# Half of the last projection tile put in front of the last attention's turning, and three conversions on other places of their queues

## The reference, cut to what matters

```python
def first_block(x, ...):                       # two layers
    for l in range(2):
        proj = rmsnorm(x, mix_norm[l]) @ w_in[l]         # retention, forgetting attention, RWKV, gates
        rwkv_c = rwkv_c + (prev - rwkv_c) * mu           # a difference with the position before
        x = x + merged(y_ret, y_fox, y_rwkv, gates) @ w_out[l]
        x = x + swiglu(rmsnorm(x, ffn_norm[l]))

def second_block(x, ...):                      # two layers, 13 groups of 256 projected columns
    for l in range(2):
        z = rmsnorm(x, norm_g[l]) @ w_in[l]
        o_a = axial rotary attention; o_b = windowed attention with a sink
        o_c = neighbourhood attention with a bias; o_d = difference of two softmaxes, rotary
        x = x + concat(o_a*silu(g_a), o_b*silu(g_b), o_c*silu(g_c), o_d*silu(g_d)) @ w_out[l]
    return rmsnorm(x, final_g)
```

## Time and profile before

| | us |
|---|---|
| median of 3 runs | 1119.23 (1119.02 to 1119.77) |
| the profiled execution | 1118.7 |
| its span in the trace | 1116.9 |
| PE busy in the span | 1102.8 |
| mean granted clock of PE | 0.997 |

### The profile page before, as it was taken

The page is one execution under the profiler, slowest core; times in us unless marked ns, Lnnn a source line. Parts: engine busy times, 40 slices in busy tenths (PEclk is TensorE's granted clock), DMA queues, the critical chain, the costliest instruction groups (busy, mean ns, idle before and its releaser), DMA issues.

```text
span 1116.9 us, 21111 instructions
## 1 busy us (share of the span) xinstructions
PE 1102.8 (99%) x8842; PEld 976.2 (87%) x8842; DVE 812.8 (73%) x1184; ACT 575.0 (51%) x858; POOL 85.3 (8%) x67
## 2 busy tenths in 40 slices
PE   9999999999999999999999999999999999999997
PEld 7789998999999998889998989999898778887786
DVE  6887664968666676888655968667677778877775
ACT  6465434444444445466444354444446676756763
POOL 1003100200000001112101200000000110002000
PEclk9999999999999999999999999999999999999998
DMA  9653335455345345443344355535345435354331
GB/s 356 233 199 102 143 116 190 152 226 226 150 190 225 136 163 218 151 152 114 115 143 168 145 227 226 208 136 220 150 150 194 155 142 187 121 197 148 115 112 38
DMA packets 29792, 188.23 MB, mean 169 GB/s; under 512 B 3537, under 2 KB 6353, under 8 KB 8337
## 3 DMA queue, kind: packets, MB, share of 16 engines
q1 hardware_dynamic: 26096, 175.63, 42.1%
q10 hardware_dynamic: 3232, 8.68, 2.1%
q0 software_dynamic: 384, 2.79, 0.7%
HBM read 181.84 MB, written 5.24 MB: 168 GB/s over the span
## 4 chain that ended last, share of the span: by engine, by line
PE 83%; issue 8%; DVE 3%; DMA 2%; ACT 2%; DVEq 1%; POOL 1%; POOLq 0%; SPq 0%; ACTq 0%
PE bank L712 14%; PE bank L772 13%; PE bank L1188 13%; PE bank L1206 10%; PE bank L1189 7%; PE bank L1165 4%; PE bank L1147 4%; DMA ring<-w_in_dram 2%; PE bank L1191 2%; PE bank L1331 1%; PE bank L864 1%; PE bank L700 1%; PE bank L727 1%; PE bank L880 1%; PE bank L903 1%
## 5 line engine op out<-in xcount | busy, mean ns | idle before, releaser
L712 PE MATMUL bank<-in_high,h_parts 128*128 128x512 f32 x544 | 177.4, 396 | 0.0
L772 PE MATMUL bank<-h_parts,in_high 128*128 128x256 f32 x768 | 144.9, 289 | 0.0
L712 PE MATMUL bank<-in_low,h_parts 128*128 128x512 f32 x336 | 131.5, 391 | 0.0
L712 PEld LDWEIGHTS bank<-in_high,h_parts 128*128 128x128 f32 x544 | 102.2, 188 | 23.9 <-issue 2.3
L772 PEld LDWEIGHTS bank<-h_parts,in_high 128*128 128x128 f32 x768 | 119.0, 191 | 3.2 <-issue 1.4
L1206 PEld LDWEIGHTS bank<-act_split,down_split 128*128 128x128 f32 x960 | 117.8, 191 | 0.9
L1206 PE MATMUL bank<-act_split,down_split 128*128 128x256 f32 x960 | 118.1, 283 | 0.0
L1188 PE MATMUL bank<-h_parts,up_split 128*128 128x512 f32 x308 | 110.6, 398 | 0.0
L1188 PE MATMUL bank<-h_parts,gate_split 128*128 128x512 f32 x308 | 110.3, 396 | 0.2
L772 PE MATMUL bank<-h_parts,in_low 128*128 128x256 f32 x384 | 108.4, 282 | 0.0
L1510 ACT ACTIVATE in_high<-ring 128x2048 fp32r<-128x2048 f32 x46 | 87.6, 1908 | 39.0 <-PE bank L712 31.9
(11 more groups left out here) (384 smaller groups left out, 2408.2 us busy)
## 6 DMA issues: line engine op xcount, KB each, us to landing
ring<-w_in_dram SPq DMA_DIRECT2D x70, 1024.0 KB, 4.9
ring<-w_gate_up_dram SPq DMA_DIRECT2D x44, 1024.0 KB, 7.7
ring<-w_down_dram SPq DMA_DIRECT2D x22, 1024.0 KB, 4.8
ring<-w_out_dram SPq DMA_DIRECT2D x16, 1024.0 KB, 4.8
ring<-p_all_dram SPq DMA_DIRECT2D x6, 1024.0 KB, 4.8
x_kept<-scratch ACTq DMA_DIRECT2D x4, 1024.0 KB, 3.9
ring<-w_in_dram SPq DMA_DIRECT2D x4, 512.0 KB, 7.2
scratch<-x_kept ACTq DMA_DIRECT2D x2, 1024.0 KB, 5.7
```

The source lines that it names most:

```text
L712: last = mm(bank[(n - n % 2 + t) % 4][:], a, b, start=c == 0 and i == 0, stop=c == KT - 1 and i == 2)
L772: last = mm(bank[g % 4][:, half * 256:(half + 1) * 256], a, b, start=k == 0 and i == 0, stop=k == KT - 1 and i == 2)
```

## The change

Four edits, all of them places in hand-written lists: in the first block, ACT's rounding of tile 5 comes behind the copies of groups 2 and 3 instead of ahead of them, and DVE's low part of tile 5 comes behind `projected_low(1)`. In the second block's third attention, a call of `piece` for blocks 0 and 1 of piece 25 is put ahead of `turn`, and the later call asks for blocks 2 to 7. In the difference attention, `out_low(2, 1)` goes to where `out_low(3, 0)` was, and `out_low(3, 0)` and `out_low(3, 1)` behind the attention; one block of piece 30 is moved behind `weigh(3)`; `next_half(0, 0)` is moved behind the low part of the last mix.

```diff
@@ PE, attend
                     weigh(3)
+                    if n == 2:
+                        piece(l, p + 4, range(2))
                     after()
                     values(1)
-                    piece(l, p + 4)
+                    piece(l, p + 4, range(2 if n == 2 else 0, KT))
@@ PE, the difference attention
                 values(2)
-                piece(l, 30, range(2))
+                piece(l, 30, range(1))
                 weigh(3)
-                piece(l, 30, range(2, 4))
+                piece(l, 30, range(1, 4))
@@ ACT, group of the first block
-                if g < 11:
+                if g < 11 and g != 3:
                     in_split(l, g + 2, ring_in, in_hi)
...
                         last.then_inc(g_out.sem, 2)
+                        if g == 3:
+                            in_split(l, g + 2, ring_in, in_hi)
@@ DVE, first block
                 projected_low(0)
-                in_split(l, 5, in_hi, in_lo)
...
                 projected_low(1)
+                in_split(l, 5, in_hi, in_lo)
@@ DVE, the difference attention
-                attention(l, att, 12, 8, 2, None, splits={1: lambda l: mixed_low(2), 5: lambda l: out_low(2, 1), 7: lambda l: out_low(3, 1)},
-                          mixing={5: lambda l: out_low(2, 0), 7: lambda l: out_low(3, 0)})
+                attention(l, att, 12, 8, 2, None, splits={1: lambda l: mixed_low(2)},
+                          mixing={5: lambda l: out_low(2, 0), 7: lambda l: out_low(2, 1)})
...
                 tt(g8, g8, put(st[:, 330:394], 1, 8), ALU.mult)
+                out_low(3, 0)
                 dve.wait_ge(*att.y.after(l, 4))
...
                 tt(y8, y8, put(st[:, 236:244], 2, HD), ALU.mult).then_inc(b_mix.sem, 1)
-                next_half(0, 0)
+                out_low(3, 1)
                 dve.wait_ge(*mx_hi.after(l, 4))
                 stt(mix_low[3][:], ...).then_inc(mx_lo.sem, 1)
+                next_half(0, 0)
                 next_half(0, 1)
```

## The result

| | before | changed |
|---|---|---|
| median, 18 runs each | 1119.12 us (1117.67 to 1119.90) | 1121.32 us (1120.62 to 1122.60) |
| profiled execution / its span | 1118.7 / 1116.9 | 1120.84 / 1119.0 |
| PE's instructions | 8842 | 8890 |

The ratio is 1.0023, with a 95% interval of 1.0017 to 1.0029: slower by 1.9 to 3.2 us. The result lies at the low end of the range that was forecast, 1121.4 to 1124.3. That range was counted from the earlier median of 1119.23: the new median is 0.08 us under it, and by the ratio the result is inside (1119.23 x 1.0023 = 1121.8). Lines of the changed kernel are a few further down: L1985 is L1989, L2020 is L2024, L2044 is L2048, L2144 is L2148, L2619 is L2623.

The account below looks back on a forecast made before the run. PE bounds the kernel, busy 1102.8 of 1116.9 us. The terms 4.38 + 0.53 - 0.18 - 0.94 - 0.07 = +3.7 us on the median 1119.23 gave 1122.95, put at 1123.0; range 1121.4 to 1124.3 for 8 in 10.

Parts of the forecast that it names:

- The bound and the sign: PE's list bounds the kernel; piece 25 computed twice adds matmuls, count 8842 to 8890, so the change is slower.
- The step that reads `token_major` as taking no blocks: Piece 25 in the third attention: both calls run the whole tile, adding 2.19 us a layer, 4.38 us in both.
- The spacing of the matmuls: Piece 25's 24 added matmuls: 2.96 us, 123 ns each by the trace; the skill's 109 ns would give 2.6 us.
- The last `weigh`: End of the difference attention: exps start 0.54 us earlier, but a block moved behind leaves a gain of 0.18 us a layer.
- The handover: First to second layer: moved `next_half(0, 0)` delays DVE's sum 1.21 us; group 1 starts 0.53 us later than before.
- nearly without idle time: DVE's sums and low parts at the next layer's start follow without pauses, so tile 1's low part ends at 978.1.
- The front: First block, copies before tile 5's rounding: the 1.44 us wait goes, 0.94 us remain won; second layer at most 0.07.
- The sum: Whole kernel: all terms together make it +3.7 us slower, 1123.0 us.
- the delay given back: Rival, last attention: its 1.9 us of waits for the mixing swallow the delay; +1.8 us, 1121.0; chance 0.05.
- the better front: Rival, first block: DVE's chain follows PE, gaining 1.44 and 0.3 us; +2.3 us, 1121.5; chance 0.12.
- The halves being halves: Rival, piece 25: the branch honours the blocks, nothing is added, the turning's waits go; 1117.4 us; chance 0.02.
- the costlier handover: Rival, next layer's first groups: the sum pushed by 1.21 us delays them in full; +0.7, 1123.7; chance 0.13.

Follow-up runs that it names:

- the edit alone: The kernel before with only the edit of piece 25, so the tile is computed twice: 1122.95 us, ratio 1.0035.
- all the others together: The changed kernel without its edit of piece 25, which runs once behind the turning as before: 1118.04 us, ratio 0.9988.
- the five traces: Traces of kernels without the first block's edit; group 4's last matmul to group 7's second took 16.29, 16.25, 16.17, 15.62 and 15.38 us.
- the real part: The changed kernel with the blocks handed on to `token_major`, so only blocks 0 and 1 run ahead of the turning: 1117.08 us, ratio 0.9985.
- two moves made differently: Against the real part: two piece 30 blocks ahead of last `weigh`, `next_half(0, 0)` ahead of last mix's low part, `out_low(3, 1)` behind `out_low(3, 0)`: 1116.36 us.

## Why the prediction was right, and where its sizes were off

**The bound and the sign.** PE's list is the path, and the doubled tile stands in it: forecast count 8890, measured 8890. The step that reads `token_major` as taking no blocks carried everything. Its price was forecast at 2.19 us a layer and 4.38 in all. The trace shows 2.12 (-0.81 to +1.31) and 2.09 (1.13, where the shift stands ahead of it, to 3.22), the edit alone +3.9 us in the time. Nothing was given back by later waits, as argued.

**The spacing of the matmuls.** "TensorE: Matmul & The Clock Gate", section "Back-to-back issue gap", in the Trainium skill gives 109 ns for an isolated gap. The trace's 2.96 us from the first doubled matmul to the turning are 123 ns each, so the measurement decides for the longer one. The section says that in a stream of weight loads and matmuls both set the spacing; here each matmul has its weight load, and no run separates their shares.

**The last `weigh`.** Forecast a gain of 0.18 us a layer; the table shows 0.36 (1.31 to 0.95) and 0.59 (3.22 to 2.63). The step that was mis-sized is the one that adds three matmuls to 1.35 us and finds 1.71 between `weigh` and `values`. It was 1.56: the 1.35 before had held some 0.15 us of waiting for ACT's copy (it ends at 960.12, and `values(3)` starts at 960.18), which the trace does not mark as idle. In the second layer DVE's mixing also lost a pause of 0.43 us inside it that the trace calls "issue"; why it went is not known. The chain itself moved by 0.57 us in the first layer, forecast 0.54.

**The handover.** Forecast +0.71 us against the shift ahead of it, measured +0.38 (0.95 to 1.33), 0.29 of it at the place itself. DVE in time, against the earlier trace rows:

```profile
967.83 2.35 DVE L2031 TENSOR_TENSOR in_low<-ring,in_high 128x1024 fp32r<-128x1024 f32 x2
970.10 1.28 DVE L2717 TENSOR_TENSOR scratch<-x,bank 128x512 f32<-128x512 f32 x2
...
976.51 2.28 DVE L2024 TENSOR_TENSOR in_low<-ring,in_third 128x2048 fp32r<-128x2048 f32 x1
```

The sum starts 1.93 us later and tile 1's low part 1.69 later; less the 0.86 that everything there had moved, 1.07 became 0.83. The claim "nearly without idle time" was the failing step: before, DVE had waited 0.66 us for PE in front of its second sum, and that pause took up part of the push, while waits for ACT at L1989 grew by 0.5 us. Ahead of the sum the push had already shrunk from the forecast 1.21 to 1.07. PE's new wait is 0.21 us, not the 0.5 to 0.7 that the prediction named.

**The front.** Forecast 0.94 and at most 0.07 us. The mechanism is in the trace: the difference no longer waits, tile 7's chain is late next and PE waits 0.56 us (forecast 0.5), and in the second layer what the difference wins is lost again at group 7 (-1.22 there, -0.93 behind). Of the 1.04 us between the two traces 0.12 stood already at group 4's last matmul and 0.91 are the edit, so for these two executions 0.94 was well forecast. It is not what the edit is worth in others: with a transfer in time it is nothing, and the mean over the five traces is 0.56. Timed alone twice, the edit gave +0.3 and -0.2 us by the ratios, each within 1.0. The failing step was to take a wait that ended on a DMA, 5.29 us for tile 5, as a fixed part of the schedule. That the gain of the first block reaches the end of the kernel is not shown by any time.

**The sum.** Forecast +3.7 us, measured +2.6 by the ratio and +2.2 by the medians. The tile edit alone measured 3.9 where 4.38 stood, and all the others together -1.3 where -0.66 stood; the intervals, 1.5 and 1.0 us to either side, exclude neither term. The trace says where the forecast was too high, up to the 2.53 us by which the last matmuls are late: 0.17 us in the tile, 0.59 at the last `weigh`, 0.33 in the handover and 0.30 in stretches that no edit touches. Against these stands 0.20 us by which the front, up to the third attention, won less than forecast. The mechanism was right at each place, and the largest errors are the sizes of the last `weigh` and of the handover.

**The rivals.** The total alone does not choose among the rivals. Measured were 1121.3 us, or 1121.8 by the ratio, both outside the 1122.0 to 1123.9 that the forecast claimed for itself and nearer to the delay given back (1121.0) and to the better front (1121.5; its own terms make it +2.5 us, 1121.7, and not +2.3). What decides is the traces. The halves being halves was built: 1117.1 us, forecast 1117.4, but for another mixture of reasons. The delay given back is ruled out by the edit alone. The better front and the costlier handover did not come.

## What to carry to other kernels

When a call is given a part of the work, follow the argument to the loop that is to obey it, for each branch; the number of instructions on the engine settles it in one line of the page. A piece of work that covers a gap often covers a second one behind it: count what waits on either side before it is moved, since here the whole tile in front cost 4.6 us more than a quarter of it, with equal work. Look at the granted clock behind new waits in windows of a few us, not at its mean over the span: it added 1.5 us to that loss. And a wait in one trace that ended on a transfer is a sample, to be looked at in a second execution before its size goes into a sum.

## What the runs showed that was not expected

- A late transfer can cost PE twice. In one execution of the kernel before, ACT stood 2.27 us in front of a tile, PE waited 1.79 us for ACT, and then PE's granted clock was 1.2 GHz for 3.4 us; the time was 1122.29 us, and the mean granted clock of 0.997 shows nothing of it.
- The last eight matmuls, L688, take 1.16 to 2.08 us behind the same wait of 0.55 us, and the moment at which the granted clock falls to 1.2 GHz goes with it. It fell at their start in the trace with 2.08 us, 0.2 us later with 1.93, some 0.4 us later with 1.76, 0.7 us later with 1.50, and after their end where they took 1.16.
- With the real part in place, two moves made differently and the second subtraction of quarter 1 in the first mixing, the kernel measured 1116.33 us, ratio 0.9977 (0.9968 to 0.9986), faster than both kernels.
